# Expert rows gated when they leave PSUM, and the last block's rows put to their tokens by TensorE

## What is computed

```python
hid = jax.nn.silu(xb @ w_gate[e]) * (xb @ w_up[e])      # 32 experts, D = 1024, 256 hidden
out = (hid @ w_down[e]).astype(jnp.float32) * buf_w[:, None]      # buf_w: the gate of a row
y = jnp.zeros((n, d), jnp.float32).at[buf_tok].add(out)           # each frame has two rows
x = x + y
return x * rsqrt(mean(x * x) + EPS) * g_final
```

## Time and profile before

| | us |
|---|---|
| median of 3 runs | 1203.12 |
| lowest and highest of the runs | 1203.11, 1205.15 |
| the profiled execution | 1198.68 |
| its span in the trace | 1196.8 |

### The profile page before, as it was taken

One profiled execution on the slowest core, in us unless ns is written; L12 is line 12 of the kernel. 1 busy time (PEld: TensorE's weight loads), 2 busy tenths in 40 slices (PEclk: granted clock), 3 DMA queues, 4 the chain that ended last, 5 costly groups with the idle time before them and its releaser, 6 DMA issues.

```text
span 1196.8 us, 19783 instructions
## 1 busy us (share of the span) xinstructions
PE 1097.5 (92%) x7553; PEld 779.2 (65%) x7553; DVE 613.8 (51%) x1631; ACT 480.7 (40%) x1036; POOL 176.5 (15%) x268
## 2 busy tenths in 40 slices
PE   5997799999999899999999899998499999999946
PEld 4984478787878798888989678787243333333312
DVE  6528978888888786723333472365421212121116
ACT  6437678787878524343343451321011111111113
POOL 1320023434342300000000000000102111111002
PEclk8999999999999999999999999999599999999978
DMA  8343140403111134232532635003889999999748
GB/s 285 50 87 64 35 102 1 114 2 84 32 51 40 34 102 123 80 99 62 142 97 80 215 106 220 38 36 129 338 320 393 419 418 418 418 420 417 291 162 340
DMA packets 127253, 205.46 MB, mean 172 GB/s; under 512 B 15108, under 2 KB 100388, under 8 KB 114868
## 3 DMA queue, kind: packets, MB, share of 16 engines
q1 hardware_dynamic: 114868, 177.63, 42.1%
q0 software_dynamic: 10560, 21.02, 5.2%
q10 hardware_dynamic: 1728, 5.51, 1.2%
HBM read 177.85 MB, written 30.18 MB: 174 GB/s over the span
## 4 chain that ended last, share of the span: by engine, by line
PE 76%; DVE 11%; ACT 4%; DMA 4%; issue 3%; POOL 1%; SPq 0%; DVEq 0%; ACTq 0%; POOLq 0%
PE psum L2498 14%; PE psum L2513 7%; PE psum L2213 5%; PE psum L2215 5%; PE psum L2214 5%; DVE place L1464 3%; PE psum L2185 2%; PE psum L2187 2%; PE psum L2186 2%; PE psum L2295 2%; PE psum L2465 2%; PE psum L2364 2%; PE psum L2366 2%; PE psum L2365 2%; PE psum L2269 2%
## 5 line engine op out<-in xcount | busy, mean ns | idle before, releaser
L2498 PE MATMUL psum<-place,place 128*32 128x512 f32 x1536 | 171.1, 597 | 1.2 <-issue 1.2
L1116 ACT ACTIVATE place<-place,place 128x768 uint8<-128x768 f32 (+3 forms) x128 | 125.6, 984 | 6.8 <-DVE place L1495 6.8
L2213 PE MATMUL psum<-place,place 128*128 128x512 f32 x288 | 121.9, 423 | 2.3 <-DVE place L1452 2.3
L2498 PEld LDWEIGHTS psum<-place,place 128*32 128x32 f32 x1536 | 49.0, 110 | 104.8 <-issue 102.3
L2215 PE MATMUL psum<-place,place 128*128 128x512 f32 x288 | 113.4, 394 | 0.0
L2214 PE MATMUL psum<-place,place 128*128 128x512 f32 x288 | 112.6, 391 | 0.0
L1910 DVE TENSOR_TENSOR place<-psum,place 128x256 f32<-128x256 f32 x24 | 10.2, 425 | 156.3 <-ACT place L1296 156.3
L2513 PE MATMUL psum<-place,place 128*32 128x512 f32 x768 | 86.9, 592 | 0.7 <-DVE place L1904 0.7
L2185 PE MATMUL psum<-place,place 128*128 128x256 f32 x288 | 84.9, 295 | 1.6 <-ACT place L1138 1.6
L2186 PE MATMUL psum<-place,place 128*128 128x256 f32 x288 | 81.4, 283 | 0.0
L2187 PE MATMUL psum<-place,place 128*128 128x256 f32 x288 | 81.4, 283 | 0.0
(11 more groups left out here) (323 smaller groups left out, 2428.3 us busy)
## 6 DMA issues: line engine op xcount, KB each, us to landing
place<-in_w_gate SPq DMA_DIRECT2D x32, 1024.0 KB
place<-in_w_up SPq DMA_DIRECT2D x32, 1024.0 KB
place<-in_w_down SPq DMA_DIRECT2D x32, 1024.0 KB
place<-in_w_in SPq DMA_DIRECT2D x28, 512.0 KB, 6.5
place<-expert_out SPq DMA_DIRECT2D x9, 1024.0 KB, 13.0
place<-in_cache_attn_k SPq DMA_DIRECT2D x32, 256.0 KB, 3.3
place<-in_cache_attn_v SPq DMA_DIRECT2D x32, 256.0 KB, 3.4
place<-in_x_prompt SPq DMA_DIRECT2D x3, 1536.0 KB, 8.6
```

Source lines behind the costliest of these rows:

```text
L1116: last = nc.scalar.activation(reached[j], score[j], ACT.Sign, bias=pivot.bitcast(F32)[:, j:j + 1], scale=-1.0, accum_out=minus[:, j - BY_A ...
L2213: nc.tensor.matmul(bank(4 + b), hT_hi[:, k, rows], hi, start=k == 0, stop=False)
L2498: last = nc.tensor.matmul(bank(b % 2)[rows], xT[b % 2][:, k, rows], w_gu[expert_of(b, q) % NSLOT][:, :, k, :], start=k == 0, stop=k == KD - 1)
```

## The change

- The gates move. DVE makes three tables in `over_slots` instead of one (`at_tables`: the old one, and the gates in two rounded parts whose sum is exact), PE's 18 products in `over_frames` get 72 columns instead of 24, and DVE takes from them `slot_gate`, the gate of each of the 128 slots of each block (`gates_of_slots`, at block 1). `rows_out` multiplies by it when it copies out of PSUM. `expert_out` then holds gated rows.
- Only blocks 0 to 22 are scattered (`NSENT` = 23). SP fills all of `expert_out` (9.4 MB) with zeros in the first head of retention, from a tile that GpSimd clears behind `q_zero`, so that a row that nobody writes reads as zero.
- The loads of `y_in` wait for the scatter of block 22 instead of 23. Tiles 6 and 7 wait for gate_up(22) and tile 8 for down(22) too, since their places hold weights.
- Block 23 is not stored: `rows_high` (ACT) and `rows_low` (DVE) split its gated rows in two float32r parts, `places` (DVE, at block 7) makes a one-hot matrix for each tile, and `put` (PE) multiplies them, four products of 128x512 for each tile, into PSUM banks.
- For tiles 1 to 7 GpSimd adds the two loaded rows of a frame (`SUM_ON_POOL`), and DVE adds that to x1; for tiles 0 and 8 DVE makes both additions (`early_sum`). In tiles 1, 3 and 5 PE adds x1 into the banks by the identity (`put_sum`); in the others DVE adds the banks to x1. For tiles 2, 4 and 6 the final scaling is one instruction of ACT and one of GpSimd (`gains`), for the others one of DVE as before. The order of tiles is 0 to 8.
- The diagonal matrices (L1320) go. The overflow loop is rewritten, and isn't entered here.

The core of the diff:

```diff
-ON_PE, LAST_ORDER = (1, 3, 5, 7), (0, 2, 1, 4, 3, 6, 5, 7, 8)
+PLACED = (NMAIN - 1,)
+NSENT = NMAIN - len(PLACED)
+SUM_ON_PE, SUM_ON_POOL, SCALE_ON_ACT = (1, 3, 5), (1, 2, 3, 4, 5, 6, 7), (2, 4, 6)
...
+        y_high = [place(y_at + D * (b % 2), D, None, F32R) for b in PLACED]
+        y_low = [place(mark_route + D * (b % 2), D, None, F32R) for b in PLACED]
+        assert top[0] <= WORDS
+
+
+        FREE_FIRST, FREE_THEN, FREE_LAST = mark_h + 2 * KD * DE, mark, mark - 2 * D
+        y_in_at = [FREE_FIRST + 2 * D * n for n in range(6)] + [FREE_THEN, FREE_THEN + 2 * D, FREE_LAST]
+        y_in = [place(at, 2 * D, "p (j d) -> p j d", j=2) for at in y_in_at]
...
+                if h == 0:
+                    sp.wait_ge(pool_set, 4)
+                    sp.dma_start(expert_out.rearrange("(n p) d -> p n d", p=P), zeros.unsqueeze(1).broadcast_to([P, 2 * T, D])).then_inc(zeroed[0], 16)
...
+            sp.wait_ge(y_out[0], 16 * ((NSENT + 1) // 2))
+            sp.wait_ge(y_out[1], 16 * (NSENT // 2))
+            for t in range(T):
+                if y_in_at[t] >= FREE_THEN:
+                    sp.wait_ge(gu_ps, NMAIN - 1)
+                if y_in_at[t] == FREE_LAST:
+                    sp.wait_ge(dn_ps, NMAIN - 1)
+                sp.dma_start(y_in[t], expert_out.rearrange("(j t p) d -> t p j d", j=2, p=P)[t]).then_inc(y_loaded(t)[0], 16)
...
+            pool.memset(zeros, 0.0).then_inc(pool_set, 1)
+            pool.wait_ge(pool_set, 4)
             pool.wait_ge(consts_late_in, 16)
...
+            pool.wait_ge(*zeroed)
+            for b in range(2, NSENT + 5):
                 if b < NMAIN:
...
+            def root(t):
                 pool.wait_ge(ssq_done, 2 * T + t + 1)
                 pool.tensor_scalar(ssq7[:, t:t + 1], ssq7[:, t:t + 1], 1.0 / D, EPS, ALU.mult, ALU.add).then_inc(ms_done, 1)
                 pool.wait_ge(ms_done, 2 * T + t + 1)
                 pool.tensor_tensor(rstd7[:, t:t + 1], ssq7[:, t:t + 1], half, ALU.pow).then_inc(rstd_done, 1)
+
+            def gains(t):
+                pool.wait_ge(*row_scaled(t))
+                pool.tensor_tensor(out_rows[t], out_rows[t], g_final, ALU.mult).then_inc(result_done(t)[0], 1)
+
+            pool.wait_ge(g_final_in, 16)
+            for t in range(T + 4):
+                if t in SUM_ON_POOL:
+                    pool.wait_ge(*y_loaded(t))
+                    pool.tensor_tensor(y_in[t][:, 0, :], y_in[t][:, 0, :], y_in[t][:, 1, :], ALU.add).then_inc(pool_set, 1)
+                if t >= 3 and t - 3 < T:
+                    root(t - 3)
+                if t - 4 in SCALE_ON_ACT:
...
+                if b == 0:
+                    act.wait_ge(frames_done, 4)
+                nc.scalar.activation(y_rows[b % 2][:, 0:512], bank(6), ACT.Copy, scale=slot_gate[:, b:b + 1]).then_inc(y_act, 1)
+
+            def rows_high(n):
+                b = PLACED[n]
+                act.wait_ge(dn_ps, b + 1)
+                if b >= 2:
+                    act.wait_ge(y_out[b % 2], 16 * ((NSENT + 1 - b % 2) // 2))
+                nc.scalar.activation(y_high[n][:, 0:512], bank(6), ACT.Copy, scale=slot_gate[:, b:b + 1]).then_inc(first_high(n)[0], 1)
+                nc.scalar.activation(y_high[n][:, 512:], bank(7), ACT.Copy, scale=slot_gate[:, b:b + 1]).then_inc(y_act, 1)
...
+            for x in range(T + 4):
                 if x < T:
-                    t = LAST_ORDER[x]
-                    if t in ON_PE:
-                        act.wait_ge(wo_ps, T + ON_PE.index(t) + 1)
-                        rows = bank(2 * ON_PE.index(t), 0, D)
+                    if x in SUM_ON_PE:
+                        act.wait_ge(wo_ps, T + x + 1)
+                        rows = last_banks(x)
                     else:
-                        act.wait_ge(x2_done, x2_after(x))
-                        rows = x1[:, t, :]
+                        act.wait_ge(*sum_added(x))
+                        rows = x1[:, x, :]
                     act.wait_ge(ssq_done, 2 * T + x)
                     nc.scalar.activation(squared, rows, ACT.Square, accum_out=ssq7[:, x:x + 1]).then_inc(ssq_done, 1)
-                if x >= 3:
-                    t = LAST_ORDER[x - 3]
-                    act.wait_ge(out_done, x - 2)
-                    act.dma_start(y_p[t * P:(t + 1) * P, :] if t < TP else y_s, out_rows[t]).then_inc(y7_out[(x - 3) % 3], 16)
+                if x - 2 in SCALE_ON_ACT:
+                    t = x - 2
+                    act.wait_ge(rstd_done, 2 * T + t + 1)
+                    nc.scalar.activation(out_rows[t], x1[:, t, :], ACT.Copy, scale=rstd7[:, t:t + 1]).then_inc(row_scaled(t)[0], 1)
+                if x >= 4:
+                    t = x - 4
+                    act.wait_ge(*result_done(t))
+                    act.dma_start(y_p[t * P:(t + 1) * P, :] if t < TP else y_s, out_rows[t]).then_inc(y7_out[t % 3], 16)
...
-                nc.vector.tensor_scalar(y_rows[b % 2][:, 512:D], bank(7), 1.0, None, ALU.mult).then_inc(y_dve, 1)
+                nc.vector.tensor_scalar(y_rows[b % 2][:, 512:D], bank(7), slot_gate[:, b:b + 1], None, ALU.mult).then_inc(y_dve, 1)
+
+            def gates_of_slots():
+
+                v.wait_ge(frames_ps, len(PARTS) + 1)
+                L(v, nc.vector.tensor_copy(slot_gate, bank(5, NOVER, NMAIN)))
+                tt(slot_gate, bank(5, NOVER + NMAIN, NMAIN), slot_gate, ALU.add).then_inc(frames_done, 1)
+                v.wait_ge(frames_done, 4)
+
+            def rows_low(n):
+
+                b = PLACED[n]
+                v.wait_ge(dn_ps, b + 1)
+                v.wait_ge(h2tr_ps, T + NMAIN)
+                for m, high in enumerate((first_high(n), (y_act, b + 1))):
+                    cols = slice(512 * m, 512 * m + 512)
+                    v.wait_ge(*high)
+                    last = nc.vector.scalar_tensor_tensor(y_low[n][:, cols], bank(6 + m), slot_gate[:, b:b + 1], y_high[n][:, cols].bitcast(F32),
+                                                          ALU.mult, ALU.subtract)
+                last.then_inc(y_dve, 1)
+
+            def places(n):
+
+                b = PLACED[n]
+                v.wait_ge(*table_sent)
+                L(v, nc.vector.tensor_copy(frame_f, block_frames[:, b:b + 1]))
+                L(v, tt(tile_frames[:, 0:T], frame_f.broadcast_to([P, T]), line_tiles[:, 0:T], ALU.subtract))
+                tt(placed_at[n], line_columns.unsqueeze(1).broadcast_to([P, T, P]),
+                   tile_frames[:, 0:T].unsqueeze(2).broadcast_to([P, T, P]), ALU.is_equal).then_inc(placed_ready(n)[0], 1)
+                v.wait_ge(*placed_ready(n))
+
+            def early_sum(t):
+
+                if t in SUM_ON_POOL:
+                    v.wait_ge(*pool_summed(t))
+                else:
+                    v.wait_ge(*y_loaded(t))
+                    L(v, tt(x1[:, t, :], y_in[t][:, 1, :], x1[:, t, :], ALU.add))
+                tt(x1[:, t, :], y_in[t][:, 0, :], x1[:, t, :], ALU.add).then_inc(x2_done, 1)
 
...
+                v.wait_ge(exp_done, 2)
+                at_over, high, low = (at_tables[:, :, :, n:n + NOVER] for n in (0, NOVER, NOVER + NMAIN))
+                L(v, nc.vector.tensor_copy(gate_high, gates))
+                L(v, tt(gate_low, gates, gate_high.bitcast(F32), ALU.subtract))
+                main, over = (C("blocks")[:, a:b].unsqueeze(1).unsqueeze(1).broadcast_to([P, 2, T, b - a]) for a, b in ((0, NMAIN), (NMAIN, NBLK)))
+                tt(high, each(slot_block, NMAIN), main, ALU.is_equal)
+                L(v, tt(at_over, each(slot_block, NOVER), over, ALU.is_equal))
+                tt(low, high.bitcast(F32), each(gate_low.bitcast(F32), NMAIN), ALU.mult)
+                L(v, tt(at_over, at_over.bitcast(F32), each(C("row").rearrange("p (j t) -> p j t", j=2), NOVER), ALU.mult))
+                tt(high, high.bitcast(F32), each(gate_high.bitcast(F32), NMAIN), ALU.mult).then_inc(slots_done, 1)
...
+                if b == 1:
+                    gates_of_slots()
+                if b >= 1 and b - 1 in PLACED:
+                    rows_low(PLACED.index(b - 1))
+                elif b >= 1:
...
+                if b - 2 >= NSLOT and b - 2 - NSLOT < len(PLACED):
+                    places(b - 2 - NSLOT)
+            early_sum(0)
+            rows_low(len(PLACED) - 1)
...
+            early_sum(1)
             for x in range(T + 2):
-                if x < T and LAST_ORDER[x] not in ON_PE:
-                    t = LAST_ORDER[x]
-                    v.wait_ge(*y_loaded(t))
-                    for j in range(2):
-                        nc.vector.scalar_tensor_tensor(x1[:, t, :], y_in[t][:, j, :], gates[:, j, t:t + 1], x1[:, t, :], ALU.mult, ALU.add).then_inc(x2_done, 1)
-                        v.wait_ge(x2_done, x2_after(x) - 1 + j)
-                if x >= 2:
-                    t = LAST_ORDER[x - 2]
-                    v.wait_ge(rstd_done, 2 * T + x - 1)
-                    rows = bank(2 * ON_PE.index(t), 0, D) if t in ON_PE else x1[:, t, :]
```

(47 more changed lines are left out.)

141 lines of the change are left out of this document (85 added, 56 removed).

## The result

The changed kernel takes 1224.66 us (median of 4 runs, 1224.23 to 1225.65) against 1203.11 for the kernel before on the same chip: ratio 1.0176, 95% interval 1.0159 to 1.0194. That is 21.55 us slower. The forecast was 15.4 slower, with a range of 1207 to 1226. The profiled execution of after took 1225.65, with a span of 1223.7.

What follows compares the result with a forecast made beforehand. PE bounds the blocks; the end is a transfer, then a chain of DVE, ACT and GpSimd. Walks with and without exclusion gave 18.4 and 12.5 us more; the middle, 1203.1 + 15.4, is 1218.5 us, range 1207 to 1226.

Steps and rivals of the forecast that it cites:

- the exclusion: DVE and GpSimd instructions hold each other up; taken as half, between 12.5 us (none) and 18.4 us (full) slower.
- the scatter's landing: Block 22's scatter was to take 4.9 us and land at 1150.5, with tile 0 landing at 1156.15.
- Part 1: Loads of the tail wait for block 22's scatter instead of block 23's, so SP issues them 4.85 us earlier.
- Part 2: Early edits (over_slots, wider products, zero fill, gates) are nearly hidden: together 0.4 us, bounds 0 to 2.
- Part 3: The tail's new chain, said to decide: ten wide GpSimd instructions of 2.39 us each, with roots 31 us in strict order.
- the walk with full exclusion: Tail streams followed in order, DVE and GpSimd fully excluding each other: last scaling 1210.6, end 1215.7, span 18.4 us above before.
- the 0.9 that was taken off: Correction to the tail walks: the same walk of the kernel before issued its last store at 1192.6, measured 1191.73.
- (a): Rival: same tail chain with cheaper meetings of DVE and GpSimd, 1207 to 1214 us; chance 0.26.
- (b): Rival: faster, early loads carry through the tail at 2.53 us a tile, about 1198.3 us median; chance 0.07.
- (d): Rival: a meeting costs more than one instruction's exclusion, or the fill lasts into the second head; above 1226, chance 0.04.

## Why the prediction was right, and where it was off

**The result** lies in the range, on the side given 0.88. The forecast was 6.2 us short. The median of before was rightly put above its profiled execution, which had the higher granted clock (0.974, against 0.968 in its second profile), and the change doesn't add to that difference. But the 6.2 us are the rest of three errors, two too low (the exclusion, the loops) and one too high (the scatter's landing), so that the range held by some luck; the right terms are below.

**Part 1.** The loads started 3.85 us behind the scatter's issue, not 4.9. The 4.90 of the earlier trace rows held 1.8 us that go with before's loops (3.10 without them). Tile 0 came 8.9 us behind the issue (1150.81 to 1159.71) where 10.5 was forecast (1145.64 to 1156.15). This was better than forecast, and it didn't matter.

**Part 2.** The fill is hidden, as said. Hidden(0)'s own time can't show the 0.4 us of the small edits, since it moves by 6.8 between two profiles of one kernel, but distances near it can. The multiplication starts 0.42 us behind the start of ACT's silu in both kernels (870.88 to 871.30, 875.04 to 875.46): over_slots just fits into the idle time. And PE's 18 products, 24 columns wide before and 72 after, take the same time:

```profile
872.04 2.16 PE L2460 MATMUL psum<-place,place 128*128 128x24 f32 x18
```

```profile
876.20 2.18 PE L2608 MATMUL psum<-place,place 128*128 128x72 f32 x18
```

So these two edits cost 0.02 us where 0.4 was put.

**Part 3.** The GpSimd instruction was taken at 2.39 and takes 2.34 (the upper bound of 2.75 works out at 2.72). The Trainium skill's figure, an estimate of 2.25 by "GPSIMD Engine Reference", section "Elementwise — side-by-side cycle accounting", lies 4% below. PE's four products for tile 0 took 2.06 where 1.9 was put; the row of 1.72 behind that is one of four products, not of two. The exclusion was put half way between none and all. It is full wherever an instruction of DVE with two tiles in SBUF meets one of GpSimd: 3.06 for 1.28, 1.05 for 0.18. This is the first term that was mis-sized: the walk with full exclusion stood in the prediction at 18.4, and it is the right one. Before the 0.9 that was taken off it has 54.5 us from tile 0's landing to the last store (1156.15 to 1210.6). The kernel without loops has 54.3 (1155.76 to 1210.10). That is no chance meeting of the ends: counted from the landing, sum 4 ends at 17.6 in both, the product of tile 2 at 34.0 in the walk and 33.8 in the trace, sum 7 at 36.4 and 36.1. After, with loops, has 59.0.

**The missing term.** The step that failed is the list of what the new order moves. The loads now run while DVE and PE pass the overflow loops, which in before lay in the wait for the first load. A loop that is not entered was costed at nothing, and with no row of its own. It costs after 6.5 us by the medians, 5.1 by the tails; before loses 3.4 and 2.2 by its loops, so that the change itself made them dearer by 3.1 and 2.9. Where they stand could have been seen in the code: DVE's loop comes behind early_sum(0) and rows_low, so behind the first load.

**The sum by the right terms**: 18.4 (full exclusion) less 2.1 (in the kernel without loops tile 0 came 8.44 us behind the scatter's issue, not 10.5) is 16.3, and that kernel has a tail 16.7 longer than before's (69.4 and 52.7). The other 5.1 of the 21.8 are the loops. They are read off the same tails, so that this last step is no check of its own; the medians put the loops at 6.5, and single tails and medians of four runs agree no better than that.

**The rivals.** (a) fell with the full exclusion. (b) named GpSimd's stream as the place, which is half of it: with that out, and the loops too, the tail is still 56.3, with DVE as the bound. Only the version that also moves additions to PE comes to 48.4. (d), above 1226, was close, by another mechanism than it named.

## What to carry to other kernels

When a transfer is moved forward, look at what each engine passes while it runs, and don't count a loop that isn't entered as nothing: keep it in a stretch in which the engine waits anyway. Two engines that exclude each other are priced as one: of a sum moved from DVE (1.22 us) to GpSimd (2.34) nothing is gained where DVE has instructions with two tiles of SBUF to run beside it, since they wait. Where an engine in strict order gets wide work in front of short steps that others wait for, walk the streams; here the walk with full exclusion was right to 0.2 us over 54.
